# Two projection blocks computed together by halves of the contraction, and modulation tiles in another order

## The chip, the cores and the metric

One NeuronCore of one Trainium2 chip. The time is the device time of one execution of the program in microseconds (us); lower is better. Everything computes in 32 bits. TensorE's matmuls are called PE below, VectorE is DVE, ScalarE is ACT, GpSimd is POOL, SyncE is SP. Only SP and POOL issue loads here, each on a DMA queue of its own.

## The reference

Two transformer-like blocks on x of 256 tokens x 2048 features. What matters here is the beginning of the first block:

```python
mod = silu(c) @ w_ada + b_ada                # one row; w_ada is 2048 x 12288
sh1, sc1, gt1, sh2, sc2, gt2 = split(mod, 6)
h = rmsnorm(x, g_norm_mix) * (1 + sc1) + sh1
proj = h @ w_in                              # 2048 x 3072
xr, gr, xp = proj in three parts of 1024
xr = causal_dwconv(xr)                       # 4 taps
hr = rg_lru(xr)                              # gates, then a scan over the tokens
y = concat([hr * gelu(gr), pool_mixer(xp)]) @ w_out
x = x + gt1 * y
```

Then follow a feed-forward network with the modulations sh2, sc2 and gt2, and the second block (attention, a state space mixer, a feed-forward network), which the change doesn't touch.

## The kernel before, in words

**Weights.** A weight matrix streams through SBUF in tiles of 1 MB (512 rows x 512 columns, buffer `raw`, four slots; SP loads them, `load_tile`). Each tile is two *halves* of 256 rows. For each half ACT rounds the weights to a high part (`split_hi`, `w_hi`), DVE takes what is left (`split_lo`, `w_lo`), and PE multiplies in 24 matmuls (`features_half`: 2 chunks of rows x 4 chunks of columns x 3 products of parts). `w_hi` and `w_lo` hold four halves (`HALF_SLOTS`), so the split of half h waits until PE has used half h-4 (`w_used`); in a block's loop, step n splits half n+3 (`LEAD`). A *block* is 512 output columns: 8 halves over the 2048 rows of the contraction. `w_in` has six blocks; they are accumulated alternately in the PSUM halves `pair[:, 0]` and `pair[:, 1]`. Halves are numbered through here: block b has halves 8b to 8b+7, half 48 is the first of `w_out`.

**Modulation.** w_ada has 12 units of 1024 columns, each 16 tiles of 128 x 1024 (0.5 MB). The first four units (sh1, sc1) are needed before the projection. SP loads their 64 tiles into eight slots, and PE multiplies each by silu(c) (`mod_product`, here a *first product*, line 1431). The four units come in the order 0, 2, 1, 3, so that the first half of the features (chunks 0 to 7 of the contraction) has its shift and scale after two units. The other 128 tiles go into a ring of six slots in the order `mod_seq`, loaded by POOL as slots become free, and are used beside the blocks. Units in `MOD_BY_PE` are multiplied by PE, two tiles at a time (here a *pair product*, line 1431 again), the others by DVE (a *product* into `mod_acc`, lines 2176 and 2180). The table `mod_places` says how many tiles belong to each *place*; place p is step p % 8 of block p // 8. DVE handles place p behind the split of half p+3; PE handles it behind half p+3.

**Beside the blocks.** Convolution taps (line 2121) read a block from PSUM, and a block two later can't start in that PSUM half before they have ended. Behind block 2 come the gates of the recurrence. In block 3 and block 4 DVE has long operations for it (2048 elements a partition; the scan among them) and the sums of the pooling windows; in block 5 the output gate, and `pool_lo`, for which the first half of `w_out` waits (`pool_lo_ev`).

**The beginning.** Behind some of the first products PE already multiplies halves of w_in: halves 0, 1, 2 behind products (2, 15), (3, 5), (3, 11), where (i, k) is tile k of unit i. These halves take chunks 0 to 5 of the contraction. Half 3 comes when all first products are done. Halves 4 to 7 take chunks 8 to 15 of the features, whose scale depends on the last first product.

## Time and profile before

| what | value |
|---|---|
| median of 3 runs | 2612.03 us (2609.85 to 2612.27) |
| the profiled execution | 2609.51 us |
| its span, first to last instruction | 2607.8 us |
| mean granted clock of PE | 0.995 of full |
| PE busy | 98% of the span |
| DVE busy | 61% |
| HBM read | 545.79 MB, 210 GB/s over the span |

The profile gives busy times by engine, waits with what ended them, and a timeline. A wait is put down to the operation that released it. Times in the trace count from the first instruction.

### The profile page before, as it was taken

The page shows a single profiled execution, that of the slowest core. Times are in us where ns is not written, and L with a number is a line of the kernel's source. Part 1 is how long each engine was busy: PE and PEld are TensorE (multiplying, and loading weights), DVE is VectorE, ACT ScalarE, POOL GpSimd, SP SyncE. Part 2 cuts the span into 40 slices and gives each one's busy share as a digit, 9 for nine tenths or more (in the row PEclk, how much of TensorE's full clock was granted, in tenths as well). Part 3 has the DMA queues.
Part 4 walks back from the last instruction along what each step waited for, and adds up shares of the span by engine and source line. Part 5 has one row for each costly group of instructions (what it writes and reads, how often), then busy time and mean ns, then how long its engine had stood idle before and what let it go on. Part 6 is the DMA issues. An engine that isn't in the chain of part 4 may idle for free.

```text
span 2607.8 us, 32728 instructions
## 1 busy us (share of the span) xinstructions
PE 2561.5 (98%) x12532; PEld 2084.6 (80%) x12532; DVE 1580.7 (61%) x1894; ACT 1264.3 (48%) x1664; POOL 73.8 (3%) x156
## 2 busy tenths in 40 slices
PE   7899999999999999999999999999999999999999
PEld 1688878888888888888877788888888888888877
DVE  1449887764545455566787686456666666644435
ACT  3344444444444444454577555445555555544453
POOL 0012210100000000000000000000000000000000
PEclk9999999999999999999999999999999999999999
DMA  9999987875555555565544534555555555555554
GB/s 383 373 350 342 360 320 253 290 232 190 190 193 185 177 190 188 187 213 171 169 127 131 163 118 163 187 193 183 188 182 188 186 184 178 188 190 188 183 205 145
DMA packets 350157, 549.45 MB, mean 211 GB/s; under 512 B 18513, under 2 KB 200801, under 8 KB 349281
## 3 DMA queue, kind: packets, MB, share of 16 engines
q1 hardware_dynamic: 331616, 480.83, 55.5%
q0 software_dynamic: 18432, 67.12, 7.0%
...
HBM read 545.79 MB, written 2.10 MB: 210 GB/s over the span
## 4 chain that ended last, share of the span: by engine, by line
PE 90%; DMA 4%; DVE 3%; ACT 1%; issue 1%; SPq 0%; POOL 0%; DVEq 0%; ACTq 0%
PE pair L1311 27%; PE pair L1313 27%; PE pair L1312 27%; DMA mod_raw<-in_w_ada 3%; DVE w_lo L1959 1%; PE pair L1886 1%; PE pair L1286 1%; PE pair L1431 1%; PE pair L1287 1%; PE pair L1288 1%; DMA raw<-in_w_in 1%; DVE mod_acc L2180 1%; PE misc L1827 1%; PE misc L1939 1%; PE misc L1327 1%
## 5 line engine op out<-in xcount | busy, mean ns | idle before, releaser
L1959 DVE TENSOR_TENSOR w_lo<-raw,w_hi 128x1024 fp32r<-128x1024 f32 x848 | 1017.5, 1203 | 844.5 <-ACT w_hi L667 842.7
L667 ACT ACTIVATE w_hi<-raw 128x1024 fp32r<-128x1024 f32 x848 | 882.8, 1043 | 1039.4 <-PE pair L1313 959.6
L1311 PE MATMUL pair<-w_hi,a_hi 128*128 128x512 f32 x2048 | 810.4, 396 | 3.3 <-DVE a_lo L2068 2.5
L1313 PE MATMUL pair<-w_hi,a_lo 128*128 128x512 f32 x2048 | 799.3, 390 | 0.0
L1312 PE MATMUL pair<-w_lo,a_hi 128*128 128x512 f32 x2048 | 798.3, 390 | 0.0
L1311 PEld LDWEIGHTS pair<-w_hi,a_hi 128*128 128x128 f32 x2048 | 385.3, 188 | 84.3 <-issue 4.2
L1313 PEld LDWEIGHTS pair<-w_hi,a_lo 128*128 128x128 f32 x2048 | 385.1, 188 | 81.4
L1312 PEld LDWEIGHTS pair<-w_lo,a_hi 128*128 128x128 f32 x2048 | 385.6, 188 | 78.0 <-issue 1.0
L1311 PE MATMUL pair<-w_hi,hid_hi 128*128 128x512 f32 x704 | 275.0, 391 | 0.0
L1313 PE MATMUL pair<-w_hi,hid_lo 128*128 128x512 f32 x704 | 274.0, 389 | 0.0
L1312 PE MATMUL pair<-w_lo,hid_hi 128*128 128x512 f32 x704 | 273.9, 389 | 0.0
L1313 PEld LDWEIGHTS pair<-w_hi,hid_lo 128*128 128x128 f32 x704 | 132.2, 188 | 27.6
L1312 PEld LDWEIGHTS pair<-w_lo,hid_hi 128*128 128x128 f32 x704 | 132.2, 188 | 27.2
L1311 PEld LDWEIGHTS pair<-w_hi,hid_hi 128*128 128x128 f32 x704 | 132.2, 188 | 26.9
L1286 PE MATMUL pair<-a_hi,w_hi 128*128 128x256 f32 x384 | 112.5, 293 | 8.9 <-DVE w_lo L1959 5.1
L1287 PE MATMUL pair<-a_lo,w_hi 128*128 128x256 f32 x384 | 109.3, 285 | 0.0
L1288 PE MATMUL pair<-a_hi,w_lo 128*128 128x256 f32 x384 | 109.2, 284 | 0.0
L1286 PEld LDWEIGHTS pair<-a_hi,w_hi 128*128 128x128 f32 x384 | 74.1, 193 | 24.0 <-issue 11.8
L2180 DVE SCALAR_TENSOR_TENSOR mod_acc<-mod_raw,keep,mod_acc 128x1024 f32<-128x1024 f32 x64 | 81.9, 1280 | 15.1 <-DMA mod_raw<-in_w_ada 14.6
L1287 PEld LDWEIGHTS pair<-a_lo,w_hi 128*128 128x128 f32 x384 | 74.3, 193 | 0.1
L1288 PEld LDWEIGHTS pair<-a_hi,w_lo 128*128 128x128 f32 x384 | 74.3, 193 | 0.0
L527 POOL DMA_DIRECT2D mod_raw<-in_w_ada x86 | 45.7, 532 | 316.2 <-DVE mod_acc L2180 127.7
...
## 6 DMA issues: line engine op xcount, KB each, us to landing
...
```

The source lines that it names most:

```text
L527: pool.dma_start(mod_slot(n), ada[:, k, bass.ds(a * MOD_COLS, MOD_COLS)]).then_inc(page_landed[mod_landing(n)[0]], 16)
L667: run(w_hi[:, h % HALF_SLOTS, 0:n, :], raw[:, h // 2 % RAW_SLOTS, at0:at0 + n, :], ACT.Copy).then_inc(hi_ready, 1)
L1286: pe.matmul(o, wh, hi[:, k, :], start=(h == kk == 0 and m % 2 == 0), stop=False, skip_group_check=True)
L1287: pe.matmul(o, wh, lo[:, k, :], start=False, stop=False, skip_group_check=True)
L1288: mm = pe.matmul(o, wl, hi[:, k, :], start=False, stop=(h == ph.halves - 1 and kk == n - 1), skip_group_check=True)
L1311: pe.matmul(o, hi[:, own], w_hi[:, slot, kk, :], start=(h == kk == 0), stop=False)
L1312: pe.matmul(o, hi[:, own], w_lo[:, slot, kk, :], start=False, stop=False)
L1313: mm = pe.matmul(o, lo[:, own], w_hi[:, slot, kk, :], start=False, stop=(h == ph.halves - 1 and kk == n - 1))
L1327: mm = pe.transpose(misc[:, m % 4 // 2, m % 2 * S + t * P:m % 2 * S + (t + 1) * P], src[:, t, m * P:(m + 1) * P], ident[:])
L1431: mm = pe.matmul(bank[own], c_silu[:, k:k + 1].to_broadcast([P, P // 4]), tile[:, e * COLS:(e + 1) * COLS], start=(k < 2), stop=(k >= KC - ...
L1959: dve.tensor_tensor(w_lo[:, slot, 0:n, :], raw[:, h // 2 % RAW_SLOTS, at0:at0 + n, :], w_hi[:, slot, 0:n, :].bitcast(F32), ALU.subtract).t ...
L2180: dve.scalar_tensor_tensor(out=acc, in0=of, scalar=by, in1=acc, op0=ALU.mult, op1=ALU.add).then_inc(mod_step, 1)
```

## The change

Four things change.

1. Blocks 0 and 1 are computed together. Halves 0 to 3 are the first four halves of block 0's contraction (chunks 0 to 7), halves 4 to 7 those of block 1; halves 8 to 11 finish block 0, halves 12 to 15 finish block 1 (`in_half`).
2. So eight halves need only the first half of the features. Six of them stand behind first products (`W_IN_AT`), two behind the last one. Four tiles of `w_in` are loaded among the 64 first tiles of w_ada instead of two. Units 2 and 3 of the first products accumulate in `misc[:, 2]`, since `pair[:, 1]` now holds block 1.
3. The convolution of block 0 runs in the second half of block 1's steps, twelve taps in three steps instead of six.
4. The later tiles come in another order. PE takes units 5 and 8 instead of 5 and 6, DVE the others. `mod_places` begins at place 9 instead of place 6, and the number of tiles at the places changes. DVE's products in blocks 2, 3, 4, 5 are 6, 8, 11, 12 instead of 4, 9, 6, 6. In w_out they are 27 instead of 32; of PE's 16 pair products 8 come in w_out instead of 2.

```diff
-    mod_places = [0] * 6 + [2, 1] * ((IN_PLACES - 8) // 2) + [2, 2] + [2, 1, 1, 1, 1, 1, 1] * 4 + [0] * 4 + [1, 0] * (4 * up1.halves)
+    mod_places = [0] * 8 + [0, 2] * 4 + [2, 1, 1, 2, 1, 1, 2, 1] * 3 + [2, 1, 1, 2, 1, 1, 2, 2] + [2, 1] * 13 + [2, 2] + [0] * 4 + [1, 0] * (4 * up1.halves)
-    MOD_BY_PE, MOD_BY_DVE = [5, 6], [4, 7, 8, 9, 10, 11]
+    MOD_BY_PE, MOD_BY_DVE = [5, 8], [4, 6, 7, 9, 10, 11]
-        order = "D" * 4 + "PPD" * 8 + "D" * 4 + "DDPP" * 8 + "D" * 32 + "D" * 32
+        order = "P" * 8 + "PPDDD" * 4 + "D" * 25 + "DPPD" * 8 + "D" * 11 + "D" * 32
...
+    def in_half(p):
+        b, h = divmod(p, w_in.halves)
+        return (b, h) if b >= 2 else (h // 4, 4 * b + h % 4)
...
+        def first_bank(i):
+            return pair[:, 1, i, :] if i < 2 else misc[:, 2, :]
...
-        TURN0_AT, W_IN_AT = [(1, 9), (1, 13), (2, 1), (2, 4)], [(2, 15), (3, 5), (3, 11)]
+        TURN0_AT, W_IN_AT = [(1, 9), (1, 13), (2, 1), (2, 4)], [(2, 12), (2, 15), (3, 2), (3, 5), (3, 8), (3, 11)]
...
             for n, (a, k) in enumerate(mod_seq):
                 if n < MOD_SLOTS_LATER:
-                    pool.wait_ge(w_used, FIRST_SPLIT - 1)
+                    pool.wait_ge(w_used, len(W_IN_AT) + 1)
...
-            w_in_at = {2 * KC + 8: 0, 3 * KC: 1}
+            w_in_at = {2 * KC + 3: 0, 2 * KC + 9: 1, 2 * KC + 15: 2, 3 * KC + 5: 3}
...
-                elif q in (XG - 3, XG - 2):
-                    split_hi(w_in, 0, [q - 1])
+                elif q > XG // 2:
+                    split_hi(w_in, 1, [q - XG // 2 - 1])
...
+                    if (b, n) == (1, 4):
+                        act.wait_ge(w_used, w_in.half(1) + 4)
+                        conv_bias(0, 0, cw1[:, (CONV - 1) * RC:], cb1, xc, c1_bias)
...
+            def half_in(p):
+                block, kh = in_half(p)
+                b, h = divmod(p, w_in.halves)
+                if b < 2:
+                    pe.wait_ge(n_lo, kh + 1)
+                features_half(w_in, b, block % 2, a_hi, a_lo, h, kh)
...
             mod_turn(MOD_ORDER[MOD_FIRST - 1], MOD_FIRST)
-            first_w_in(3)
+            for h in range(len(W_IN_AT), w_in.halves):
+                first_w_in(h)
...
-            split_lo(w_in, 0, [0, 1])
+            split_lo(w_in, 0, range(4))
             first_result(2)
-            split_lo(w_in, 0, [2, 3])
+            split_lo(w_in, 0, range(4, w_in.halves))
...
-                if b in (1, 2):
-                    conv_taps(n, (b - 1) % 2, 4 * (b - 1), cw1, CONV, RC, xc, c1_bias, c1_tap, 12 * (b - 1))
+                if b == 1 and 4 <= n < 7:
+                    for place in (2 * n - 8, 2 * n - 7):
+                        conv_taps(place, 0, 0, cw1, CONV, RC, xc, c1_bias, c1_tap, 0)
+                elif b == 2:
+                    conv_taps(n, 1, 4, cw1, CONV, RC, xc, c1_bias, c1_tap, 12)
```

The order on PE behind the first w_in half of the beginning: x8 of line 1431 are four first products, and the matmul of `w_hi` that follows is the first of 24. Before:

```order
L1288 MATMUL pair<-a_hi,w_lo 128x256
L1431 MATMUL pair<-mod_raw,keep 32x512 x8
L1423 MATMUL misc<-keep,mod_rows 128x2 x4
L1431 MATMUL pair<-mod_more_78,keep 32x512 x4
L1286 MATMUL pair<-a_hi,w_hi 128x256
```

After:

```order
L1300 MATMUL pair<-a_hi,w_lo 128x256
L1436 MATMUL misc<-mod_more_78,keep 32x512 x2
L1436 MATMUL misc<-mod_more_79,keep 32x512 x4
L1298 MATMUL pair<-a_hi,w_hi 128x256
```

A half now follows after three first products instead of six.

The order on DVE where block 4 begins, from its first split (`w_lo`, of half 35) to that of half 38; `mod_acc` are the products of modulation tiles. Before:

```order
L2180 SCALAR_TENSOR_TENSOR mod_acc<-mod_page,keep,mod_acc 128x1024
L1959 TENSOR_TENSOR w_lo<-raw,w_hi 128x1024
L2279 TENSOR_TENSOR lru_u<-lru_u,lru_m 128x2048
L2281 MEMSET lru_a 128x8
L2180 SCALAR_TENSOR_TENSOR mod_acc<-mod_page,keep,mod_acc 128x1024
L1959 TENSOR_TENSOR w_lo<-raw,w_hi 128x1024
L2284 SCALAR_TENSOR_TENSOR xc<-lru_a,lru_u 128x2048
L2186 TENSOR_TENSOR mod<-misc,vec 128x8
L1959 TENSOR_TENSOR w_lo<-raw,w_hi 128x1024
```

After:

```order
L2190 SCALAR_TENSOR_TENSOR mod_acc<-mod_raw,keep,mod_acc 128x1024 x2
L1969 TENSOR_TENSOR w_lo<-raw,w_hi 128x1024
L2290 TENSOR_TENSOR lru_u<-lru_u,lru_m 128x2048
L2292 MEMSET lru_a 128x8
L2186 TENSOR_SCALAR mod_acc<-mod_raw,keep 128x1024
L1969 TENSOR_TENSOR w_lo<-raw,w_hi 128x1024
L2295 SCALAR_TENSOR_TENSOR xc<-lru_a,lru_u 128x2048
L2190 SCALAR_TENSOR_TENSOR mod_acc<-mod_raw,keep,mod_acc 128x1024
L2196 TENSOR_TENSOR mod<-misc,vec 128x8
L1969 TENSOR_TENSOR w_lo<-raw,w_hi 128x1024
```

Four products stand here instead of two.

The order on DVE at the end of block 5, up to the last `pool_lo`. Before:

```order
L1959 TENSOR_TENSOR w_lo<-raw,w_hi 128x1024
L2180 SCALAR_TENSOR_TENSOR mod_acc<-mod_raw,keep,mod_acc 128x1024
L1959 TENSOR_TENSOR w_lo<-raw,w_hi 128x1024
L2331 SCALAR_TENSOR_TENSOR pool_lo<-misc,vec,pool_hi 128x256 x3
L1959 TENSOR_TENSOR w_lo<-raw,w_hi 128x1024
L2331 SCALAR_TENSOR_TENSOR pool_lo<-misc,vec,pool_hi 128x256 x3
L2180 SCALAR_TENSOR_TENSOR mod_acc<-mod_raw,keep,mod_acc 128x1024 x2
L1959 TENSOR_TENSOR w_lo<-raw,w_hi 128x1024
L2331 SCALAR_TENSOR_TENSOR pool_lo<-misc,vec,pool_hi 128x256 x2
```

After:

```order
L1969 TENSOR_TENSOR w_lo<-raw,w_hi 128x1024
L2190 SCALAR_TENSOR_TENSOR mod_acc<-mod_page,keep,mod_acc 128x1024
L1969 TENSOR_TENSOR w_lo<-raw,w_hi 128x1024
L2342 SCALAR_TENSOR_TENSOR pool_lo<-misc,vec,pool_hi 128x256 x3
L2186 TENSOR_SCALAR mod_acc<-mod_raw,keep 128x1024
L1969 TENSOR_TENSOR w_lo<-raw,w_hi 128x1024
L2342 SCALAR_TENSOR_TENSOR pool_lo<-misc,vec,pool_hi 128x256 x3
L2190 SCALAR_TENSOR_TENSOR mod_acc<-mod_raw,keep,mod_acc 128x1024 x2
L1969 TENSOR_TENSOR w_lo<-raw,w_hi 128x1024
L2190 SCALAR_TENSOR_TENSOR mod_acc<-mod_raw,keep,mod_acc 128x1024
L2190 SCALAR_TENSOR_TENSOR mod_acc<-mod_page,keep,mod_acc 128x1024
L2342 SCALAR_TENSOR_TENSOR pool_lo<-misc,vec,pool_hi 128x256 x2
```

Three more products stand ahead of the last `pool_lo`.

## Rows read from the trace of the kernel before

**Rows 1.** Page, part 1: busy time, share of the span, instructions.

```profile
PE 2561.5 (98%) x12532; PEld 2084.6 (80%) x12532; DVE 1580.7 (61%) x1894; ACT 1264.3 (48%) x1664; POOL 73.8 (3%) x156
```

**Rows 2.** Waits of PE, whole span: what for, us in total, times, longest.

```profile
PE pair L1431 <- DMA mod_raw<-in_w_ada: 10.3, 19, 2.9
...
PE pair L1431 <- DMA mod_more<-in_w_ada: 7.5, 12, 2.9
...
PE pair L1286 <- DVE w_lo L1959: 5.1, 5, 1.8
...
PE pair L1311 <- DVE pool_lo L2331: 1.3, 1, 1.3
```

**Rows 3.** Timeline of PE, 97 to 107 us: start, us, engine, line, operation [idle before].

```profile
97.91 2.15 PE L1431 MATMUL pair<-mod_more,keep 128*32 128x512 f32 x16
...
101.67 0.36 PE L1286 MATMUL pair<-a_hi,w_hi 128*128 128x256 f32 x1
...
106.58 0.39 PE L1286 MATMUL pair<-a_hi,w_hi 128*128 128x256 f32 x1 [1.80 <-DVE w_lo L1959]
```

**Rows 4.** Busy us of each engine in two stretches, clock, DMA share, GB/s.

```profile
80.00:90.00 10.00, 9.38 (x55) 4.52 (x52) 2.43 (x3) 1.88 (x2) 0.00 (x0) 1.00 1.03 411
...
240.00:260.00 20.00, 18.56 (x141) 15.88 (x140) 19.79 (x27) 6.25 (x8) 4.27 (x9) 1.00 0.93 319
```

**Rows 5.** Timeline of PE, 128 to 280 us.

```profile
128.11 0.28 PE L1286 MATMUL pair<-a_hi,w_hi 128*128 128x256 f32 x1
...
130.99 0.28 PE L1286 MATMUL pair<-a_hi,w_hi 128*128 128x256 f32 x1
...
134.95 0.39 PE L1286 MATMUL pair<-a_hi,w_hi 128*128 128x256 f32 x1
...
148.28 0.39 PE L1286 MATMUL pair<-a_hi,w_hi 128*128 128x256 f32 x1 [3.25 <-DVE xc L2121]
...
152.85 1.06 PE L1431 MATMUL misc<-mod_page,keep 128*32 128x512 f32 x8
...
206.76 0.39 PE L1286 MATMUL pair<-a_hi,w_hi 128*128 128x256 f32 x1 [1.50 <-DVE w_lo L1959]
...
212.62 0.28 PE L1286 MATMUL pair<-a_hi,w_hi 128*128 128x256 f32 x1
...
253.87 0.39 PE L1286 MATMUL pair<-a_hi,w_hi 128*128 128x256 f32 x1 [0.48 <-DVE w_lo L1959]
...
279.06 0.50 PE L1311 MATMUL pair<-w_hi,pool_hi 128*128 128x512 f32 x1 [1.27 <-DVE pool_lo L2331]
```

**Rows 6.** Timeline of ACT at 145 us.

```profile
145.14 2.00 ACT L667 ACTIVATE w_hi<-raw 128x1024 fp32r<-128x1024 f32 x2 [12.89 <-DMA raw<-in_w_in]
```

**Rows 7.** Timeline of DVE, 216 to 254 us.

```profile
216.67 2.35 DVE L1959 TENSOR_TENSOR w_lo<-raw,w_hi 128x1024 fp32r<-128x1024 f32 x2
...
236.55 1.28 DVE L2180 SCALAR_TENSOR_TENSOR mod_acc<-mod_raw,keep,mod_acc 128x1024 f32<-128x1024 f32 x1
...
237.74 1.22 DVE L1959 TENSOR_TENSOR w_lo<-raw,w_hi 128x1024 fp32r<-128x1024 f32 x1
...
238.88 0.17 DVE L2260 COPY pool_b<-pool_a 128x12 f32<-128x12 f32 x1
...
252.60 1.21 DVE L1959 TENSOR_TENSOR w_lo<-raw,w_hi 128x1024 fp32r<-128x1024 f32 x1
```

**Rows 8.** Waits of DVE, 219 to 253.8 us, and 253.9 to 279.1 us.

```profile
DVE mod_acc L2180 <- DMA mod_page<-in_w_ada: 2.8, 1, 2.8
...
DVE mod_acc L2180 <- DMA mod_raw<-in_w_ada: 4.6, 4, 1.7
...
DVE w_lo L1959 <- ACT w_hi L667: 0.4, 1, 0.4
```

**Rows 9.** Timelines of PE and of DVE, 282 to 288 us.

```profile
282.00 1.06 PE L1431 MATMUL misc<-mod_page,keep 128*32 128x512 f32 x8
...
287.38 0.75 DVE L2176 TENSOR_SCALAR mod_acc<-mod_page,keep 128x1024 f32<-128x1024 f32 x1 [1.29 <-DMA mod_page<-in_w_ada]
```

More of the change, by code:

```diff
@@ L579, in _, with load_in @@
             sp.dma_start(c_rows[0:KC, :], by_chunk(d["c"][0])).then_inc(c_landed, 16)
-            w_in_at = {2 * KC + 8: 0, 3 * KC: 1}
+            def load_in(b, j):
+                block, h = in_half(w_in.halves * b + 2 * j)
+                k0 = w_in.half_rows(h)[1]
+                load_tile(w_in, b, j, plain(d["w_in"][0], bass.ds(w_in_cols[block], COLS)), k0)
+            w_in_at = {2 * KC + 3: 0, 2 * KC + 9: 1, 2 * KC + 15: 2, 3 * KC + 5: 3}
             for s in range(MOD_FIRST * KC):
@@ L592, in _ @@
                 if s in w_in_at:
-                    load_tile(w_in, 0, w_in_at[s], plain(d["w_in"][0], bass.ds(w_in_cols[0], COLS)))
-            for j in range(len(w_in_at), w_in.tiles):
-                load_tile(w_in, 0, j, plain(d["w_in"][0], bass.ds(w_in_cols[0], COLS)))
+                    load_in(0, w_in_at[s])
             for b in range(1, w_in.blocks):
@@ L604, in _ @@
                     sp.dma_start(pool_w[:], d["w_pool"][0].rearrange("g (k p) n -> p (g k) n", p=P)).then_inc(mixw_landed, 16)
-                load(w_in, b, plain(d["w_in"][0], bass.ds(w_in_cols[b], COLS)))
+                for j in range(w_in.tiles):
+                    load_in(b, j)
             for b in range(w_out.blocks):
@@ L864, in _ @@
                     first_out(2)
-                    split_hi(w_in, 0, [2, 3])
+                    split_hi(w_in, 0, range(2, w_in.halves))
                     first_out(3)
-                elif q in (XG - 3, XG - 2):
-                    split_hi(w_in, 0, [q - 1])
+                elif q > XG // 2:
+                    split_hi(w_in, 1, [q - XG // 2 - 1])
             def mixer(b):
@@ L1284, in features_half @@
                         wh, wl = (w[:, slot, kk, m * P:(m + 1) * P] for w in (w_hi, w_lo))
-                        pe.matmul(o, wh, hi[:, k, :], start=(h == kk == 0 and m % 2 == 0), stop=False, skip_group_check=True)
+                        pe.matmul(o, wh, hi[:, k, :], start=(kh == kk == 0 and m % 2 == 0), stop=False, skip_group_check=True)
                         pe.matmul(o, wh, lo[:, k, :], start=False, stop=False, skip_group_check=True)
-                        mm = pe.matmul(o, wl, hi[:, k, :], start=False, stop=(h == ph.halves - 1 and kk == n - 1), skip_group_check=True)
+                        mm = pe.matmul(o, wl, hi[:, k, :], start=False, stop=(kh == ph.halves - 1 and kk == n - 1), skip_group_check=True)
                 mm.then_inc(w_used, 1)
-            def features(ph, b, c, hi, lo, beside=None, before=None, first=0):
-                for h in range(first, ph.halves):
-                    features_half(ph, b, c, hi, lo, h, before)
-                    if beside:
-                        beside(h)
             def tokens(ph, b, c, operand, beside=None, before=None):
@@ L1506, in pools @@
                     mm.then_inc(pool_mm, 1)
-            for b in range(w_in.blocks):
-                if b == 1:
-                    pe.wait_ge(mod_ready, MOD_FIRST)
-                elif 2 <= b < 4:
+            pe.wait_ge(mod_ready, MOD_FIRST)
+            for b in range(1, w_in.blocks):
+                if 2 <= b < 4:
                     pe.wait_ge(c1_tap, 12 * (b - 1))
@@ L1515, in _ @@
                     pe.wait_ge(xp_ev, b - 3)
-                def beside_w_in(h):
-                    if b == 0 and h == 4:
-                        pe.wait_ge(mod_ready, MOD_FIRST)
-                        mods_beside(0)
+                for h in range(w_in.halves):
+                    half_in(b * w_in.halves + h)
                     mods_beside(b * w_in.halves + h - LEAD)
@@ L1522, in beside_w_in @@
                         pools(h)
-                features(w_in, b, b % 2, a_hi, a_lo, beside_w_in, normed_yet(0) if b == 0 else None, 4 if b == 0 else 0)
                 if b == 2:
@@ L2333, in pooled_out @@
                                              op0=ALU.mult, op1=ALU.subtract).then_inc(pool_lo_ev, 1)
-            for b in range(w_in.blocks):
+            for b in range(1, w_in.blocks):
                 mixer(b)
```

54 lines of the change are left out of this document (24 added, 30 removed).

## The prediction

> **What bounds the kernel now.** I read the page first: PE is busy 98% of the span [rows 1], so the time is PE's work plus PE's waits, and the change can only move waits. The view of PE's waits says where they are [rows 2]: 17.8 us for the first products' tiles (the DMA bounds the beginning), 5.1 us for `w_lo`, 1.3 us for `pool_lo`, and in the timeline 3.25 us for the convolution [rows 5]. Then I read PE's timeline around them. The first products end at 97.91 + 2.15 = 100.06; half 3 starts at 101.67, half 4 at 106.58 after a wait [rows 3]. The DMA moves 411 GB/s in that stretch [rows 4]. Afterwards a half starts every 2.88 us (128.11 to 130.99), and a pair product beside it makes 3.96 of that, so a pair costs 1.08 [rows 5]. Half 16 (block 2) starts at 148.28 after a wait of 3.25 for the taps of block 0, and then takes 4.57 us instead of some 2.9, about 1.6 us lost to a lower clock (by a fine look at its matmuls, most of them start at twice the usual distance) [rows 5]. Those taps were late because DVE stood behind a split whose tile had not landed: ACT waited 12.89 us for it until 145.14 [rows 6]. Last I looked at who is full where: from 240 to 260 DVE is busy 19.79 of 20 us [rows 4]. So there are two regimes: DMA at the beginning, DVE in blocks 4 and 5.
>
> **The change, step by step.** The sum is made against the profiled execution's 2609.51 us.
>
> *Beginning.* Two more tiles of 1 MB go in front of the last tile of w_ada: 2.1 MB at 411 GB/s, 5.1 us [rows 4]. PE does three more halves in that stretch; they lie beside the loads. After the last of them come four products as before, but PE now works three products and one half (1.6 + 2.9 = 4.5 us) against 3.8 us of their loads plus half a tile (1.3), so it is nearly full and I add 0.4: the first products end at 105.6. `mod_turn` behind them takes what it did (1.6), so half 6 starts at 107.2. Before, half 3 started at 101.67.
>
> *Halves 6 to 15.* Ten halves at 2.88 and two pairs at 1.08 are 31.0: half 16 could start at 138.2. Halves 6 and 7 (5.8 us) now cover the chain mod, scale, a_hi, a_lo, w_lo that took 106.58 - 101.67 = 4.9 us [rows 3]. I add 0.5 for the splits that alternate with it, so half 16 starts at 138.7 if its taps and its tile are there. The taps: block 0 is complete behind half 11, at about 124.7; bias, three splits and twelve taps then take 10 us (an estimate: three splits at 1.14 [rows 7], twelve taps of a quarter of a split's elements at 0.4 each, and 2 for the bias), to 135. The tile: between the last tile of w_ada and it lie 4 MB of w_in, 1.5 MB of gate and pool weights, itself, and POOL's six tiles, 10 MB, 24.3 us at 411 GB/s; with some 2 us for the small pieces it lands at 131, and the split chain behind it ends at 138. Just in time. Gain at half 16: 148.28 - 138.7 = 9.6, and 1.6 of clock, 11.2.
>
> *Blocks 2 and 3.* The same halves, and as many pairs (six). The wait of 1.50 at half 30 [rows 5] stood behind DVE's products of block 3, of which one fewer remains, and I take it as gone. From half 16 to half 32 it was 212.62 - 148.28 = 64.3; less 1.6 and 1.5 it is 61.2. Half 32 starts at 199.9, 12.7 earlier.
>
> *Block 4.* Here DVE sets the pace. From the end of its split of half 35 (216.67 + 2.35 = 219.02, which is 6.4 behind the start of half 32) to that of half 43 (252.60 + 1.21 = 253.81) it took 34.8 us [rows 7], 2.8 of them waiting for a tile [rows 8], with six products. A product takes 1.19 start to start, a split 1.14 [rows 7]. Eleven products: 34.8 - 2.8 + 5 x 1.19 - 0.5 (one is the shorter first product of a unit) = 37.4. I let it start 6.6 behind half 32, since a pair product behind half 27 frees the slots for the products of step 4, which is late for DVE just as a pair was before. So half 43 starts at 199.9 + 6.6 + 37.4 = 243.9, against 253.87: 10.0 gained. PE waits about 9 us in this block, where it waited 1.5.
>
> *Block 5.* From 253.81 to the last `pool_lo` (where half 48 starts, 279.06) DVE took 25.2 [rows 5, 7], with 4.6 + 0.4 = 5.0 of waits [rows 8]: six more products make 25.2 - 5.0 + 6 x 1.19 - 0.5 = 26.8. PE needs 21.8 (its 25.2 less 1.27 less two pairs), so it waits 5 us for `pool_lo`. Half 48 starts at 270.7, 8.4 earlier.
>
> *What is owed.* By then PE has done 8 pair products, before 14. The six cost 6 x 1.08 = 6.5 later, in w_out. That leaves 1.9.
>
> *Two more losses.* A wait of 5 us is longer than the 3.25 behind which the clock fell; I take the same 1.6. And in w_out, in the last step of blocks 0, 1 and 2 there, DVE's product waits for a slot that a pair product frees three halves before PE needs the split behind it. A pair that began at 282.00 let DVE's product start at 287.38, 4.3 us after the pair's end [rows 9]; with the product, two additions of the same size as a split, and the split: 4.3 + 1.2 + 2.4 + 1.15 = 9.1 against 3 x 2.88 = 8.6 of cover. Half a microsecond three times, 1.5; the bounds are nothing (the slot comes 0.5 earlier) and 2 us each time. The rest of the program is the same.
>
> Sum: 1.9 - 1.6 - 1.5 = 1.2 us slower, 2610.7 on the profiled execution's scale. The median of the runs is 2.5 above that execution, so I forecast a median of 2613, which is no change that can be told: a measurement here tells 0.2%, 5.2 us. The bounds of the unknown terms, added roughly: beginning and tile -2 to +5, entry into block 4 -3.4 to +2, clock 0 to 3, w_out 0 to 6.
>
> **The rivals.** *DVE is not so full (faster, 2604).* If the products' tiles are there in block 3, DVE enters block 4 with all the lead that four `w_hi` slots allow: the split of half 35 ends some 3.2 behind half 32, not 6.6, which gives 3.4. If the clock holds as well behind the `pool_lo` wait (1.6) and the slots in w_out come in time (1.5), and PE's pair products fit into waits, it is 6 to 9 us better than the sum. For it: DVE had 7.8 us of tile waits in blocks 4 and 5 [rows 8], which fewer pair products there would remove anyway. Against it: most of that I have already taken off. It decides at a split of half 35 within 3.3 us of half 32.
>
> *The tile of block 2 stays late (slower, 2620).* Before, it landed at 145.14 [rows 6], behind the gate weights. If it comes at 136 instead of 131, PE waits 5 us before half 16 and the clock falls again, 1.6: 2613 + 6.6 = 2620. For it: SP issues it behind the small gate loads, and POOL's six tiles start at the same time. Against it: these gate loads can be issued 10 us earlier relative to PE. It decides at a landing after 132.
>
> *The clock falls in block 4 (slower, 2619).* PE would wait 1 to 3 us before each of six halves. In this trace waits of 1.50 and 0.48 left the clock at its upper level and 3.25 didn't [rows 5]. Were it lowered through these halves, each would cost 1.6 more, of which its wait of about 1.5 hides most, but the last, the pools and block 5 are not hidden: 4 to 8 us. The Trainium skill (TensorE: Matmul & The Clock Gate, HAM oscillation) says that a kernel whose matmul bursts are short against its waits runs every burst cold; by it this would be the likelier case. Here the bursts are 2.9 us and the waits 1 to 3, so the row of 1.50 speaks against it.
>
> *The change does not do what it says*: no sign; the order shows the halves moved.
>
> **How the numbers follow.** Forecast (the gain of the beginning is spent in blocks 4 to 6): 0.47, its own range 2607 to 2618. DVE not so full: 0.29. Tile late: 0.13. Clock in block 4: 0.11. So within 0.2% of 2612.03 (2606.8 to 2617.2) 0.46, faster 0.30, slower 0.24. The range 2602 to 2622 takes in the three rivals.
>
> **What would show it.** First products end at 105 to 106 us; no wait for `w_lo` or `xc` between halves 6 and 16; half 16 near 138.7; half 32 near 200; then waits for `w_lo` at halves 38 to 43, 7 to 11 us in sum; half 43 near 244; a wait for `pool_lo` of 4 to 6 us before half 48, near 270.7; DVE over 95% busy in block 4. The forecast is wrong if half 32 is not some 12 us earlier, or if PE waits under 5 us for `w_lo` in block 4, or if PE's waits up to half 48 and behind it differ in sum from before's by more than 5 us.

## The result, and the profile after

The changed kernel takes 2615.93 us (median of 12 runs, 2612.94 to 2618.36); the kernel before, in 12 runs beside it, 2609.12 us (2605.41 to 2612.27). The ratio is 1.0024 with a 95% interval of 1.0016 to 1.0033: 0.24% slower, about 6 us, with most of the interval beyond the 0.2% that the prediction had called no change that can be told. The profiled execution took 2616.21 us, its span is 2614.5 us, and before's was 2607.8.

Engine totals, page part 1, changed kernel:

```profile
PE 2561.7 (98%) x12532; PEld 2085.2 (80%) x12532; DVE 1580.8 (60%) x1894; ACT 1264.6 (48%) x1664; POOL 73.8 (3%) x156
```

Against [rows 1] nothing moved by more than 0.6 us: the same work in the same busy time, so what changed is when the work runs: the waits, and how work overlaps or meets a low clock. Waits of PE over the span, changed kernel (us in total, times, longest):

```profile
PE pair L1298 <- DVE w_lo L1969: 9.3, 7, 2.9
PE pair L1436 <- DMA mod_more<-in_w_ada: 8.1, 10, 2.8
PE pair L1436 <- DMA mod_raw<-in_w_ada: 5.4, 8, 2.3
PE pair L1316 <- DVE pool_lo L2342: 5.3, 1, 5.3
PE misc L1436 <- DMA mod_raw<-in_w_ada: 3.8, 5, 2.9
...
PE pair L1316 <- DVE w_lo L1969: 2.5, 4, 0.8
...
PE misc L1436 <- DMA mod_more<-in_w_ada: 1.9, 1, 1.9
```

Against [rows 2]: slightly more waiting for first tiles (19.2 in the four lines of L1436, two of which write `misc` now, where there was 17.8), no wait for the convolution, but 9.3 for `w_lo` where there was 5.1, 5.3 for `pool_lo` where there was 1.3, and 2.5 for `w_lo` in the lines of w_out and behind it. All waits of PE together are 46.4 us, where before had 39.9. The timeline of PE says when (start, us, engine, line, operation, idle before; the rows are the first matmul of halves 4 and 5, the last four first products, then halves 6, 16, 32, 38, 39, 43 and 48, the last waits of w_out, and the first half of up1):

```profile
97.70 0.39 PE L1298 MATMUL pair<-a_hi,w_hi 128*128 128x256 f32 x1
...
102.60 0.39 PE L1298 MATMUL pair<-a_hi,w_hi 128*128 128x256 f32 x1
...
105.66 1.92 PE L1436 MATMUL misc<-mod_more,keep 128*32 128x512 f32 x16
...
109.24 0.36 PE L1298 MATMUL pair<-a_hi,w_hi 128*128 128x256 f32 x1
...
140.96 0.28 PE L1298 MATMUL pair<-a_hi,w_hi 128*128 128x256 f32 x1
...
201.03 0.28 PE L1298 MATMUL pair<-a_hi,w_hi 128*128 128x256 f32 x1
...
222.56 0.39 PE L1298 MATMUL pair<-a_hi,w_hi 128*128 128x256 f32 x1 [1.42 <-DVE w_lo L1969]
...
228.55 0.39 PE L1298 MATMUL pair<-a_hi,w_hi 128*128 128x256 f32 x1 [2.85 <-DVE w_lo L1969]
...
245.80 0.39 PE L1298 MATMUL pair<-a_hi,w_hi 128*128 128x256 f32 x1 [1.60 <-DVE w_lo L1969]
...
272.61 0.79 PE L1316 MATMUL pair<-w_hi,pool_hi 128*128 128x512 f32 x1 [5.26 <-DVE pool_lo L2342]
...
363.76 0.50 PE L1316 MATMUL pair<-w_hi,pool_hi 128*128 128x512 f32 x1 [0.27 <-DVE w_lo L1969]
372.30 0.47 PE L1316 MATMUL pair<-w_hi,lru_hi 128*128 128x512 f32 x1 [0.78 <-DVE w_lo L1969]
381.98 0.50 PE L1316 MATMUL pair<-w_hi,lru_hi 128*128 128x512 f32 x1 [0.68 <-DVE w_lo L1969]
...
392.91 0.77 PE L1316 MATMUL pair<-w_hi,a_hi 128*128 128x512 f32 x1 [2.52 <-DVE a_lo L2078]
```

Set these beside [rows 5]: half 16 starts 7.3 us earlier than before (140.96 against 148.28), half 32 11.6 earlier, half 43 8.1 earlier, half 48 6.45 earlier (272.61 against 279.06), and up1 starts 7.1 *later* (392.91; before, the same row stands at 385.77). So nearly half of the gain at half 32 was spent by half 48, and between half 48 and up1 the changed kernel took 120.3 us where before took 106.7. Behind up1 little differs: the changed kernel is 7.1 us late there and 6.7 us late at the end of the span.

ACT at the tile of block 2, changed kernel, answers to [rows 6] (145.14):

```profile
133.33 1.06 ACT L679 ACTIVATE w_hi<-raw 128x1024 fp32r<-128x1024 f32 x1 [3.17 <-DMA raw<-in_w_in]
```

Busy time of each engine in block 4's first halves, in the stretch of PE's waits for `w_lo`, and up to half 48 (PE, PEld, DVE, ACT, POOL; clock, DMA share, GB/s):

```profile
201.00:220.00 19.00, 19.00 (x162) 19.00 (x161) 18.79 (x14) 10.36 (x9) 3.18 (x6) 1.00 1.02 392
220.00:246.00 26.00, 16.98 (x131) 15.80 (x130) 25.75 (x34) 8.54 (x8) 4.23 (x8) 1.00 0.72 252
246.00:272.00 26.00, 21.34 (x152) 20.30 (x151) 25.58 (x27) 9.56 (x14) 5.83 (x11) 0.99 1.00 368
```

DVE is busy 70.1 of 71 us from half 32 to half 48, while PE falls to 17.0 of 26 and the DMA to 252 GB/s. In this stretch it is DVE, and not the loads, that is full.

### The profile page after: what moved, and what is told of

Same layout as the page of the kernel before. It is cut to its first block, busy times and chain, and to the rows that moved or that the text cites. A ratio compares the mean times of both kernels' runs of the same rounds, so it can differ in the third digit from the quotient of the medians.

```text
span 2614.5 us, 32736 instructions
## 1 busy us (share of the span) xinstructions
PE 2561.7 (98%) x12532; PEld 2085.2 (80%) x12532; DVE 1580.8 (60%) x1894; ACT 1264.6 (48%) x1664; POOL 73.8 (3%) x156
## 4 chain that ended last, share of the span: by engine, by line
PE 90%; DVE 5%; DMA 2%; issue 1%; ACT 1%; SPq 0%; POOL 0%; DVEq 0%; ACTq 0%
PE pair L1316 27%; PE pair L1318 26%; PE pair L1317 26%; DMA mod_raw<-in_w_ada 2%; DVE mod_acc L2190 2%; PE misc L1436 1%; PE pair L1298 1%; DVE w_lo L1969 1%; PE pair L1299 1%; PE pair L1300 1%; PE pair L1896 1%; PE misc L1837 1%; PE misc L1949 1%; PE misc L1332 1%; PE misc L1669 0%
```

## The experiments

All runs are read with one table. "Half 16", "half 48" and "up1" are the starts of these halves on PE in each profile; "pairs" are the pair products that PE had done when half 48 started; the ratio is to the kernel before on the same chip.

| run | half 16 | half 48 | 16 to 48 | pairs | up1 | 48 to up1 | ratio (95%) |
|---|---|---|---|---|---|---|---|
| before | 148.3 | 279.1 | 130.8 | 14 | 385.8 | 106.7 | 1 |
| changed | 141.0 | 272.6 | 131.7 | 8 | 392.9 | 120.3 | 1.0024 (1.0016 to 1.0033) |
| b1_new_tiles | 145.7 | 276.5 | 130.8 | 8 | 396.0 | 119.6 | 1.0031 (1.0019 to 1.0043) |
| a3_old_tiles | 145.7 | 278.0 | 132.3 | 14 | 386.3 | 108.3 | 0.9986 (0.9977 to 0.9995) |
| a2_halves_apart | 167.4 | 298.7 | 131.2 | 8 | 418.2 | 119.5 | 1.0116 (1.0097 to 1.0135) |
| a4_short_products | 140.2 | 257.2 | 117.0 | 8 | 374.1 | 116.9 | 0.9953 (0.9935 to 0.9972) |
| b2_short_products | 147.9 | 275.4 | 127.5 | 14 | 381.9 | 106.5 | 0.9990 (0.9979 to 1.0001) |
| a1_pairs_kept | 140.8 | 268.1 | 127.3 | 11 | 389.1 | 121.0 | 1.0003 (0.9994 to 1.0011) |
| a5_pairs_spread | 140.3 | 270.2 | 129.9 | 13 | 386.2 | 116.0 | 0.9987 (0.9978 to 0.9996) |
| a6_pairs_and_early | 140.7 | 286.3 | 145.6 | 13 | 398.1 | 111.9 | 1.0043 (1.0029 to 1.0056) |
| a7_early_pairs | 140.5 | 271.6 | 131.1 | 8 | 401.4 | 129.8 | 1.0051 (1.0036 to 1.0066) |
| a8_early_pairs_sums_later | 140.4 | 271.8 | 131.3 | 8 | 389.4 | 117.6 | 1.0014 (1.0004 to 1.0023) |
| a9_spread_pairs_first | 139.9 | 269.8 | 129.9 | 13 | 381.9 | 112.1 | 0.9986 (0.9977 to 0.9995) |

Kernels with the same beginning start half 16 between 139.9 and 141.0, so differences under about a microsecond are not read.

My theory, T: the beginning gains, and the gain is spent because DVE's products fill DVE in blocks 4 and 5 and because pair products left undone (owed) have to be done in w_out. Rivals: the tiles' landings set the pace there (R1); DVE's load only moves into w_out (R2); the beginning's gain never reaches half 48 (R3).

**a4_short_products** takes DVE's load away and keeps every tile that is loaded and waited for. It shortens the products in blocks 4 and 5 to 64 of 1024 columns, except the first of a unit, and so leaves out part of the modulation:

```
 of, by, acc = mod_slot(n), c_silu[:, k:k + 1], mod_acc[:, MOD_BY_DVE.index(a) % 2, :]
+if sum(mod_places[:32]) <= n < sum(mod_places[:48]) and k:
+    of, acc = of[:, 0:64], acc[:, 0:64]
```

> The changed kernel with DVE's products at places 32 to 47 (blocks 4 and 5) over the first 64 columns of a tile only, but for a unit's first: that part of the modulation is left out, waits and loads stay. Theory (DVE): the waits of 9.0 for w_lo and 5.3 for pool_lo go, half 48 starts at 257 to 259, the clock stays up, median 2597 to 2600. Rival (tiles or the DMA): waits of 5 us or more for w_lo or pool_lo stay in blocks 4 and 5, median 2606 to 2614.

Measured: 2597.96 us. Waits of PE for `w_lo` over the whole of w_in, and no wait for `pool_lo` at all (where 9.3 and 5.3 stood):

```profile
PE pair L1298 <- DVE w_lo L1969: 0.5, 2, 0.3
```

From half 16 to half 48 it took 117.0 instead of 131.7, and half 48 came at 257.2, inside what T gave. Tiles and weights came in time for a PE that runs 15 us ahead, so R1 is out for the changed kernel: its waits in blocks 4 and 5 are DVE's time. (Shorter products also free slots sooner, which this run alone can't set apart; but from half 32 to half 48 of the changed kernel DVE is busy 70.1 of 71 us and has no wait for a tile.)

**b2_short_products** makes the same cut in the kernel before.

> The kernel before with DVE's products at places 32 to 47 over the first 64 columns only, but for a unit's first (that part of the modulation is left out). With the same cut in the changed kernel (18.4 us gained in the span's half 48 and the clock) it says how near DVE already was to being the bound. Theory (there was little slack, and little was lost): PE's waits between halves 32 and 48 in before, 2.7 us, go: median 2606 to 2608. Rival (DVE paced the kernel before in these blocks as well): more than 6 us faster, below 2604.

Measured: 2606.8 us; 16 to 48 shorter by 3.3 us. So DVE's products cost the kernel before some 3 us between halves 16 and 48 and the changed one 14.7, and the difference is what its new order of tiles did there. The time alone does not tell this run from the kernel before (the interval ends at 1.0001); the 3.3 are read from the traces.

**b1_new_tiles** and **a3_old_tiles** split the change. b1 is the kernel before with the changed table alone (the places of sums and results move with the table, not shown):

```
-mod_places = [0] * 6 + [2, 1] * ((IN_PLACES - 8) // 2) + [2, 2] + [2, 1, 1, 1, 1, 1, 1] * 4 + [0] * 4 + [1, 0] * (4 * up1.halves)
-MOD_BY_PE, MOD_BY_DVE = [5, 6], [4, 7, 8, 9, 10, 11]
-order = "D" * 4 + "PPD" * 8 + "D" * 4 + "DDPP" * 8 + "D" * 32 + "D" * 32
+mod_places = [0] * 8 + [0, 2] * 4 + [2, 1, 1, 2, 1, 1, 2, 1] * 3 + [2, 1, 1, 2, 1, 1, 2, 2] + [2, 1] * 13 + [2, 2] + [0] * 4 + [1, 0] * (4 * up1.halves)
+MOD_BY_PE, MOD_BY_DVE = [5, 8], [4, 6, 7, 9, 10, 11]
+order = "P" * 8 + "PPDDD" * 4 + "D" * 25 + "DPPD" * 8 + "D" * 11 + "D" * 32
```

> The kernel before with the changed kernel's order of tiles alone (blocks 0 and 1 one after the other, three halves among the first products, as before). With the run of the old tiles in the joined blocks it splits the gain at half 16 (148.3 before, 141.0 changed, 145.7 joined with the old tiles) into its two parts. Theory (the tile of block 2 came late because DVE's early products emptied slots and so called more w_ada tiles down beside it): here it lands by 136, half 16 starts without the wait of 3.25 and at full clock at 144 to 146, so that the quiet start gives some 4 + 1.6 and the joining some 4. Then blocks 4 and 5 are paced by DVE as in the changed kernel: median 2617 to 2621. Rival (the joining alone brought the tile forward): half 16 at 147 to 149 behind a wait of 3 or more, median over 2621.

a3 is the changed kernel with the old table, two places later (units, sums and results follow, not shown):

```
-mod_places = [0] * 8 + [0, 2] * 4 + ...
+mod_places = [0] * 8 + [2, 1] * 20 + [2, 2, 1, 1, 1, 1, 1] * 4 + [0] * 4 + [1, 0] * (4 * up1.halves)
-order = "P" * 8 + "PPDDD" * 4 + "D" * 25 + "DPPD" * 8 + "D" * 11 + "D" * 32
+order = "D" * 4 + "PPD" * 8 + "D" * 4 + "DDPP" * 8 + "D" * 32 + "D" * 32
```

> The joined blocks of the changed kernel with the order of tiles of the kernel before, begun two places later (place 8), its sums and results two places later too; four tiles more lie in w_out. Theory (the joining gains 7 us at half 16, and the new order of tiles loses it): half 16 at 141 to 142, half 48 at 271 to 272.5 as in the changed kernel but with 13 or 14 pair products done instead of 8, so median 2609 - 7 = 2602 (2600 to 2606). Rival (DVE's products beside the joined blocks delay splits and taps, which is why they were taken away there): half 16 starts at 145 or later behind a wait, median 2607 to 2612.

Measured: b1 2619.13 us, a3 2607.43 us. The first rows are b1's (ACT at the tile of block 2, then PE's half 16), the second a3's:

```profile
136.27 1.06 ACT L667 ACTIVATE w_hi<-raw 128x1024 fp32r<-128x1024 f32 x1 [3.25 <-DMA raw<-in_w_in]
...
145.65 0.28 PE L1286 MATMUL pair<-a_hi,w_hi 128*128 128x256 f32 x1
```

```profile
139.07 1.06 ACT L679 ACTIVATE w_hi<-raw 128x1024 fp32r<-128x1024 f32 x1 [8.50 <-DMA raw<-in_w_in]
...
145.69 0.58 PE L1298 MATMUL pair<-a_hi,w_hi 128*128 128x256 f32 x1 [5.34 <-DVE xc L2130]
```

The four kernels make a square: with and without the joining of blocks 0 and 1, with the old and with the new table. Block 2's tile lands at 145.1 (neither part), 139.1 (joined only), 136.3 (new tiles only), 133.3 (both). So both parts bring it forward, and a3's rival was the right one for its half 16. In a3 DVE has started five products by 134 us, their slots empty early, and POOL issues four more w_ada tiles between 124 and 131 us, beside the weights; the changed kernel does none of these products and issues no w_ada tile between 115.6 and 131.4. The tile is late, the taps behind its split are late, and PE waits 5.34. The new table has no product of DVE in blocks 0 and 1; I call that the quiet start. With it alone (b1) the wait is gone and half 16 is 2.6 earlier than before and at full clock; joining adds 4.7 to that, of which up to 1.5 is the clock, since half 4 of b1 took 4.64 us and that of the changed kernel 3.13. At the other end the time goes with the table: 1.0031 and 1.0024 with the new one, 0.9986 and 1 with the old. **Joining alone, with the old table, is the better half of the change**: 0.14% faster than before. That joining also gains with the new table (1.0024 against 1.0031) the times do not separate; in the two profiles up1 starts 3.1 us earlier with the joining.

**a2_halves_apart** meant to take only the joining out of the changed kernel:

```
 def in_half(p):
     b, h = divmod(p, w_in.halves)
-    return (b, h) if b >= 2 else (h // 4, 4 * b + h % 4)
+    return b, h
-TURN0_AT, W_IN_AT = [(1, 9), (1, 13), (2, 1), (2, 4)], [(2, 12), (2, 15), (3, 2), (3, 5), (3, 8), (3, 11)]
+TURN0_AT, W_IN_AT = [(1, 9), (1, 13), (2, 1), (2, 4)], [(2, 15), (3, 3), (3, 7), (3, 11)]
-w_in_at = {2 * KC + 3: 0, 2 * KC + 9: 1, 2 * KC + 15: 2, 3 * KC + 5: 3}
+w_in_at = {2 * KC + 8: 0, 3 * KC: 1, 3 * KC + 8: 2, 3 * KC + 15: 3}
```

> The changed kernel, but block 0's halves one after another and then block 1's, as before the change; four halves stand among the first products (a fifth needs the normalized features that the last first unit scales). The new tile order stays. Theory (joining by halves is worth the wait behind the fourth half, about 5 us, less the taps' earlier input, and that lead is handed on through DVE-bound blocks): half 16 at 144 to 147 (changed kernel 141.0), half 48 3 to 5 later than 272.6, median 2619 to 2621. Rival (blocks 4 and 5 are paced by DVE from a time that does not depend on the beginning): half 48 at 272 to 274, median 2615 to 2617.

Measured: 2640.34 us, 24 us above the changed kernel, where the theory had 3 to 5 and the rival about none. My kernel was at fault: the order of splits was made for joined blocks. DVE's next `a_lo` stands behind the split of a half whose `w_hi` slot only the waiting half frees, so halves 4 to 7 went one at a time, and at the lower clock besides, which is some 7 of the 26 us by which half 16 is late (PE, halves 4, 6 and 48; "issue" is time in which the profile shows no releaser):

```profile
111.55 0.55 PE L1298 MATMUL pair<-a_hi,w_hi 128*128 128x256 f32 x1 [2.67 <-issue]
...
129.04 0.55 PE L1298 MATMUL pair<-a_hi,w_hi 128*128 128x256 f32 x1 [3.70 <-issue]
...
298.66 0.79 PE L1316 MATMUL pair<-w_hi,pool_hi 128*128 128x512 f32 x1 [5.27 <-DVE pool_lo L2342]
```

It says nothing of the joining, but it settles R3. Half 16 was 26.5 us later than in the changed kernel (167.4), half 48 was 26.1 later, with the same wait for `pool_lo`. Lateness at half 16 is handed to half 48 in full; the stretch between takes the 131 us that its table gives. b1 shows the same on a smaller scale: 4.7 us later at half 16, 3.9 at half 48. So the 7.3 us of the beginning were real at half 48 too, and the order of tiles took back the rest: 131.7 us with eight pairs done, where before took 130.8 with fourteen and with 1.6 of low clock in it.

**a1_pairs_kept** moves four pairs from w_out into blocks 4 and 5 and eight of DVE's products out of them, the number of tiles at each place unchanged:

```
-order = "P" * 8 + "PPDDD" * 4 + "D" * 25 + "DPPD" * 8 + "D" * 11 + "D" * 32
+order = "P" * 8 + "PPDDD" * 4 + "D" * 2 + "DDPPDDPPDDD" + "DDPPDDDPPDDD" + "D" * 9 + "PP" + "D" * 10 + "DPPD" * 3 + "D" * 10 + "D" * 32
-SUMS_AT, RESULT_AT = {..., 49: 6, ...}, {..., 53: 6, ...}
+SUMS_AT, RESULT_AT = {..., 51: 6, ...}, {..., 54: 6, ...}
```

> The changed kernel with four of the eight pair products of unit 8 moved from w_out into blocks 4 and 5 of w_in, and eight of DVE's products moved from there into w_out; the number of tiles at each place stays (sums of unit 6 two places later). Theory (DVE's products set the pace of blocks 4 and 5): DVE has 8 x 1.19 = 9.5 us less there, PE four pairs (4.3) more, which fall into its waits of 9.0 + 5.3; half 48 starts at 264 +- 2 instead of 272.6, with no wait over 2 and no low clock behind it (2.9), and w_out has four pairs (4.4) less: 16 us less by the end of w_out if DVE keeps up there, a median of 2600 to 2604, 0.3% below the kernel before. Rival (the tiles' landings set the pace there, DVE only waits with them): the waits stay, half 48 at 271 to 273, median 2611 to 2616. Rival (DVE full in w_out instead): half 48 at 264, but waits for w_lo of 5 us or more in w_out, median 2606 to 2610.

Measured: 2610.64 us, back to before's time, but 7 us above the slow end of T's range. The waits for `w_lo` in w_in fell from 9.3 to 2.5; the wait for `pool_lo` did not go. PE and DVE in this run:

```profile
268.06 0.73 PE L1316 MATMUL pair<-w_hi,pool_hi 128*128 128x512 f32 x1 [4.83 <-DVE pool_lo L2342]
...
261.44 1.28 DVE L2190 SCALAR_TENSOR_TENSOR mod_acc<-mod_raw,keep,mod_acc 128x1024 f32<-128x1024 f32 x1 [3.33 <-DMA mod_raw<-in_w_ada]
```

DVE was no longer full; it stood 3.3 us in front of a product whose tile had not come, with a split and the pooled features queued behind. By the order of tiles this one takes the slot of the second tile of a pair that PE read at 254.50 to 255.56, and the tile was there 5.9 us after that, at 261.44. A pair at a place is read by PE about three halves after DVE has passed that place, and the tiles stream through six slots in one order. T had priced the pairs in blocks 4 and 5 at nothing but PE's time; they have this second price. DVE waited so once more, 6.1 us until 282.36, and PE behind it 2.9 before the half at 284.93. And from half 48 to up1 it took 121.0 us though three pairs fewer were left: besides the 2.9 and a low clock behind it, PE waited 3.8 us for the last addition to `x_res` at the end of w_out, where the changed kernel waits 0.6. That is R2 in part. So R1 is wrong for the changed kernel but true, by way of the slots, once DVE has room.

**a5_pairs_spread** goes the other way and gives each block of w_in the same number of tiles:

```
...
+mod_places = [0] * 8 + [0, 2] * 4 + [2, 1] * 16 + [2, 1, 1, 2, 1, 1, 2] * 4 + [0] * 4 + [1, 0] * (4 * up1.halves)
+order = "P" * 8 + "PPD" * 2 + "DDPPDD" + "PP" + "D" * 10 + "DDPP" * 8 + "D" * 32 + "D" * 32
+ROWS_AT, SUMS_AT, RESULT_AT = {28: 5, 72: 8}, {26: 5, 32: 4, 51: 6, 65: 7, 71: 8}, {31: 5, 36: 4, 55: 6, 69: 7}
```

> The changed kernel's joined blocks and its quiet start (four pair products and no product of DVE at places 8 to 15), then twelve tiles a block: 6, 10, 6 and 6 products for DVE in blocks 2 to 5 (changed kernel 6, 8, 11, 12) and 14 pair products done before half 48 (8), so two pairs and 36 products of DVE in w_out (8 and 27). Theory (the gain of the beginning is real and is lost only by DVE's load in blocks 4 and 5 and by the owed pairs): half 16 at 141, waits for w_lo in block 4 below 4 in sum, half 48 at 266 to 269 with a wait for pool_lo below 3, and w_out 6 shorter for its pairs: median 2599 to 2605, 0.2 to 0.4% below before. Rival (DVE is full in w_out with 36 products): waits for w_lo over 5 us in w_out, 2606 to 2610. Rival (PE's later reading of pairs holds the slots, and DVE waits for tiles): over 10 us of waits for tiles on DVE in blocks 4 and 5 and PE waits over 5 there, 2606 to 2612.

Measured: 2608.5 us, 0.13% faster than before, 3.5 us above T's range. The wait for `pool_lo` (2.41) came as T said; those for `w_lo` in block 4 were 4.1 where T had said below 4, half 48 came at 270.2 where T had 266 to 269, and it ran at the lower clock for 1.6 us, which T had left out. DVE's waits for tiles in blocks 4 and 5 were 7.1 us, under the 10 of the second rival. What was left is R2, though at another wait than the one it named: DVE busy 39 of 40 us in the middle of w_out, and PE waits at its end for the last addition to `x_res`:

```profile
310.00:350.00 40.00, 39.98 (x192) 33.04 (x191) 38.99 (x35) 14.44 (x18) 10.05 (x19) 1.00 1.03 400
...
380.08 0.45 PE L1332 MATMUL misc<-ident,x_res 128*128 128x128 f32 x1 [5.66 <-DVE x_res L2373]
```

**a9_spread_pairs_first** puts the last two pairs of that kernel in front of w_out's products:

```
...
-"DDPP" * 8 + "D" * 32 + "D" * 32
+"DDPP" * 6 + "PPPP" + "D" * 36 + "D" * 32
```

(the sums of unit 6 at place 53, its result at 57)

> The run with the pairs spread (a median 2.2 us below before's there), with the last two pairs' tiles at the front of w_out instead of among DVE's first eight products, sums and result of unit 6 two places later. Theory (slots that a pair holds starve DVE at 270 to 300, where it waited 7.8 us for tiles in four waits, and it is then full until PE's 5.7 us wait for x_res): with the pairs in front DVE waits once, the total of its tile waits behind half 48 falls below 5, and the wait for x_res to 1 to 4: 2 to 4 us below that run against before, so 0.2 to 0.3% below before. Rival (36 products at 1.5 a place fill DVE at the end whatever came before): wait for x_res of 5 to 7, ratio 0.998 to 0.9995 as there.

Measured: 2605.29 us, ratio 0.9986. In the trace the wait for `x_res` fell from 5.66 to 2.44 and w_out took 112.1 instead of 116.0, though the tile waits of DVE behind half 48 stayed at 7.6 in sum (6.2 of it in one, where T had said below 5), now at a point where DVE has time:

```profile
286.86 1.28 DVE L2190 SCALAR_TENSOR_TENSOR mod_acc<-mod_raw,keep,mod_acc 128x1024 f32<-128x1024 f32 x1 [6.17 <-DMA mod_raw<-in_w_ada]
...
375.77 0.45 PE L1332 MATMUL misc<-ident,x_res 128*128 128x128 f32 x1 [2.44 <-DVE x_res L2373]
```

Of the 3.9 us, 1.6 are not the edit's: the first half of w_out ran at full clock here (3.03 us) and at the lower one in a5 (4.61), behind waits of 2.52 and 2.41. The ratio missed the 0.2 to 0.3% of the theory; by the times the run is not told apart from a5 (0.9987) or from a3 (0.9986). These three beat the kernel before by about 0.14%.

**a6_pairs_and_early** gave blocks 3 and 5 two more tiles each, for DVE, and w_out 32 products (6, 12, 6 and 8 in blocks 2 to 5):

```
+mod_places = [0] * 8 + [0, 2] * 4 + [2, 1] * 4 + [2, 2, 1, 2, 2, 1, 2, 2] + [2, 1] * 4 + [2, 1, 2, 2, 2, 1, 2, 2] + [2, 2, 1, 1, 1, 1, 1] * 4 + [0] * 4 + [1, 0] * (4 * up1.halves)
+order = "P" * 8 + "PPDPPDDDPPDD" + "PP" + "D" * 12 + "DDPP" * 3 + "DDPP" * 3 + "DD" + "PPDD" * 2 + "D" * 28 + "D" * 32
```

> As the run with the pairs spread, but with two tiles more in block 3 and two more in block 5, all for DVE: 6, 12, 6 and 8 products in blocks 2 to 5 and 32 in w_out (36 there), the pairs as there. Theory (with the pairs spread the loss was DVE, full in w_out until PE's 5.7 us wait for x_res at its end, while it had room in block 3): that wait falls below 1.5 and the clock behind it stays up, waits for w_lo up to half 48 stay below 5 in sum, median 3 to 6 us below that run's: 2602 to 2605, 0.2 to 0.3% below before. Rival (DVE's products of block 3 push into block 4, since the loads or the slots do not come faster): half 48 at 272 or later, median as that run's or above, 2608 to 2612.

Measured: 2620.63 us, above the theory's range and the rival's. The wait for `x_res` went as hoped (0.6) and w_out was the shortest of the joined kernels with the quiet start, 111.9, but half 16 to half 48 took 15.7 us more than in a5. The rows are DVE's and PE's at the end of block 5:

```profile
267.15 1.28 DVE L2190 SCALAR_TENSOR_TENSOR mod_acc<-mod_raw,keep,mod_acc 128x1024 f32<-128x1024 f32 x1 [7.85 <-DMA mod_raw<-in_w_ada]
...
270.42 3.78 PE L1519 MATMUL misc<-xp,pool_w 128*128 128x256 f32 x8 [4.96 <-DVE pool_lo L2342]
...
277.42 1.06 PE L1436 MATMUL misc<-mod_page,keep 128*32 128x512 f32 x8
...
282.68 1.28 DVE L2190 SCALAR_TENSOR_TENSOR mod_acc<-mod_page,keep,mod_acc 128x1024 f32<-128x1024 f32 x1 [7.29 <-DMA mod_page<-in_w_ada]
...
286.26 0.80 PE L1316 MATMUL pair<-w_hi,pool_hi 128*128 128x512 f32 x1 [7.78 <-DVE pool_lo L2342]
```

Held slots again, and twice. The product at 267.15 stands behind the slot of a pair that PE read until 262.38: 7.85 us of waiting on DVE, and 4.96 on PE at the next step of the pools. The one at 282.68, right in front of the last pooled features, stands behind the pair that PE read from 277.42: 7.29 us on DVE and 7.78 on PE. With 6.3 us for `w_lo` PE waited 19.1 us between halves 32 and 48, where a5 has 6.5. A table has to keep the product that follows pairs by six tiles away from DVE's urgent work.

**a7_early_pairs** and **a8_early_pairs_sums_later** ask what made the waits in the last block of w_out in the changed kernel. Both draw unit 8's pairs together:

```
...
-"DPPD" * 8 + "D" * 11
+"DPP" * 8 + "D" * 19
```

> The changed kernel with unit 8's eight pairs in the first 24 tiles of w_out instead of 32, so that DVE has 19 products in a row behind them instead of 12. The waits in question are the changed kernel's 2.5 us for w_lo in w_out, all in its last block (0.27, 0.78, 0.68), behind a wait of DVE for a tile of 7.35 us at 355.2. Theory (slots that a pair holds make DVE late): DVE's longest wait for a tile behind half 64 falls below 4 and PE's waits for w_lo there fall below 1; median 2613 to 2616. Rival (the rate of 1.5 products a place fills DVE there whatever came before): longer waits, 2.5 to 6 us, in the last two blocks, median 2616 to 2620.

Measured: 2622.42 us, by an error in my table: unit 7's last product had moved behind its sums, and PE waited 7.08 us for it. The mended one (sums of unit 7 at place 66, result at 71):

> The run with early pairs again, but the sums of unit 7 four places later (66; its last product stands at 65, and in that run PE waited 7.1 us for it behind half 65, which was the table's fault) and its result at 71. The question is the same: what makes DVE late in the last block of w_out in the changed kernel (PE's waits of 0.27, 0.78 and 0.68 there). Slots held by pairs: waits below 1 in sum behind half 64 and a longest tile wait of DVE below 4, median 2613 to 2616. The rate of 1.5 products a place: waits of 1.0 to 2.5 in the last block whatever came before (0.32 and 0.71 stood there in the run with early pairs, even behind its idle 7 us), median 2614 to 2618.

Measured: 2612.82 us, ratio 1.0014. DVE's waits for tiles from 345 to 385 us and PE's for `w_lo` from 272 to 385 us, first in the changed kernel, then in this one:

```profile
DVE mod_acc L2190 <- DMA mod_raw<-in_w_ada: 7.8, 2, 7.4
...
PE pair L1316 <- DVE w_lo L1969: 1.7, 3, 0.8
```

```profile
DVE mod_acc L2190 <- DMA mod_raw<-in_w_ada: 1.2, 1, 1.2
...
PE pair L1316 <- DVE w_lo L1969: 0.7, 1, 0.7
```

The long tile wait went and two of PE's three waits with it, though DVE has as many products at 1.5 a place in that block (PE's waits for `x_res` behind it rose from 0.6 to 1.5). So these waits came from slots that pairs hold. The third, 0.7 us near 380, stands in all kernels with 1.5 products a place there; that it is DVE's rate is argued, not shown.

## Why the prediction was right, and where it was short

The forecast was 2613 us and "no change that can be told"; it came out 2615.93 us and 0.24% slower, inside the range and just over that line. The mechanism held at each stage that I had named; the sum was 1.2 us of loss where the trace has 7.1 at up1. That 2613 lies within 3 us of the result is partly luck: it was counted from a median of 2612.03 us in three runs, and twelve runs gave the same kernel 2609.12. The steps:

- *Beginning*: first products end at 105.6, half 6 at 107.2. Measured 107.58 (105.66 + 1.92) and 109.24. The term "three products and one half, 1.6 + 2.9 = 4.5" is the one mis-sized; the loads, which the prediction let set the pace here, did not set it, since from half 0 (76.94) to the end of the first products PE never waited. Halves 4 and 5 are 4.90 apart (97.70, 102.60) with nothing but three products between. A product beside a half costs (4.90 - 2.88) / 3 = 0.67, not 0.53, and five such groups are the 2 us.
- *Halves 6 to 15*: half 16 at 138.7, no wait for taps, tile landing at 131, "just in time". Measured 140.96, no wait, ACT starts on the tile at 133.33. Right apart from the 2.0 handed on. I had given the order of tiles no part in this; b1 and a3 show that without the quiet start the tile comes at 139 and half 16 at 145.7.
- *Blocks 2 and 3*: half 32 at 199.9, measured 201.03; one of the two us won back.
- *Block 4*: waits of about 9 us for `w_lo` (7 to 11), half 43 at 243.9. Measured 9.0 in six waits, before halves 38 to 43 as said, and half 43 at 245.80; a4 shows that these are DVE's products.
- *Block 5*: a wait of 5 us, half 48 8.4 earlier. Measured 5.26, and 6.45 earlier.
- *What is owed*: six pairs, 6.5 us. In the trace a half of w_out with a pair beside it is 3.81 behind the one before, and one without 2.72, so a pair costs what was said.
- *Clock behind the wait for `pool_lo`*: taken as 1.6 from the 3.25 before half 16; measured 2.9. Fourteen matmuls of w_out started 0.43 us apart instead of 0.23 (272.61 to 278.6). These ran at the lower of the two levels, 1.2 GHz; I had copied the loss from another wait and another kind of half.
- *w_out*: 1.5 us for three slot waits in the last steps of its blocks 0 to 2. Measured 4.2: w_out took 13.6 us longer than before, less 6.5 and 2.9. The mechanism (slots freed late behind a pair) was right, a8 shows it, but the place was wrong: DVE does wait 5 to 7 us for a tile three times in the first two blocks (until 296.1, 307.7 and 326.2), and PE has no wait for `w_lo` behind them; the price falls due in the last block, where DVE waits 7.35 us at 355.2 and then has products at 1.5 a place and no time to recover; PE's waits of 0.27, 0.78 and 0.68 there cost more than themselves, since the overlap of matmuls breaks too (372.30 is 3.81 behind the half before it, where before has 2.85: 0.78 of wait and 0.2 more). Some 1.7 us of the 4.2 lie in differences under half a microsecond that I did not trace further.

The forecast had half 48 8.4 us earlier and it came 6.45 earlier: 1.9 handed on from the beginning. With 1.3 of clock and 2.7 of w_out that makes the 5.9 us between 1.2 and 7.1.

One sign of being wrong that the prediction had set was met: PE's waits differ by 6.5 us in sum from before's, where it allowed 5. It was badly set, since the forecast's own waits (9 and 5 in blocks 4 and 5 and 1.5 in w_out, for 9.3 removed) already come to 6.2. The other two signs were not met.

Of the rivals, *DVE is not so full* is refuted by 25.75 of 26 us. *The tile of block 2 stays late* did not happen in the changed kernel: the tile came behind the point of decision that I had set (133.3 against 132), but half 16 was itself 2.3 late and met it without a wait. It is what a3 does. *The clock falls in block 4* did not happen in the profile of the changed kernel. It did in the profiles of four kernels with the same waits: behind 2.85 to 2.87 us before half 39, that half took 4.3 to 5.5 us instead of 3.1 in b1, a2, a7 and a8. So the row of 1.50 on which I set this rival aside bears on the shorter waits only. The Trainium skill (TensorE: Matmul & The Clock Gate, HAM oscillation) describes a matmul kernel whose bursts are shorter than the waits between them and all run cold. The prediction called this rival the likelier case by that, and read the page too widely: here the six waits are 0.9 to 2.9 us and the bursts about 3. No burst of the six ran cold in the changed kernel, and in those four only the one behind the longest wait did, so no trace here shows the page's case.
